# Second block's queries and keys with both input parts as one 512-column operand, and a sum of two banks behind it

## The reference, cut to what matters

```python
h = rms_norm(x, pre_mix_g[l])
z = h @ w_in[l]
za, zb, zc = z[..., :split_a], z[..., split_a:split_b], z[..., split_b:]
ya = spatial_gating(...)                 # from za
q, k, v = jnp.split(zb, 3, axis=-1)      # 512 columns each
yb = moba_attention(q, k, v)             # one block of 256 keys: causal attention with ALiBi
yc = conformer_conv(zc, w_dw[l], ...)    # gated, then a depthwise convolution with 31 taps
y = jnp.concatenate([ya, yb, yc], axis=-1) @ w_out[l]
```

## Time and profile before

| | |
|---|---|
| median of 3 runs | 783.48 us (783.41 to 783.9) |
| the profiled execution | 783.46 us, its span 782.2 us, so 1.26 us around the span |
| PE busy | 769.6 us, 98% |
| PEld, DVE, ACT, POOL busy | 85%, 73%, 56%, 9% |
| mean granted TensorE clock | 0.999 of full speed |

### The profile page before, as it was taken

The page is one execution under the profiler, slowest core; times in us unless marked ns, Lnnn a source line. Parts: engine busy times, 40 slices in busy tenths (PEclk is TensorE's granted clock), DMA queues, the critical chain, the costliest instruction groups (busy, mean ns, idle before and its releaser), DMA issues.

```text
span 782.2 us, 11452 instructions
## 1 busy us (share of the span) xinstructions
PE 769.6 (98%) x4454; PEld 668.2 (85%) x4454; DVE 569.1 (73%) x785; ACT 438.5 (56%) x660; POOL 70.4 (9%) x128
## 2 busy tenths in 40 slices
PE   6999999999999999999999999999999999999996
PEld 5999877888898888888899997789988888888885
DVE  5987999779696666686667998657647656665664
ACT  5555687674665444444465477656646744444452
POOL 4033720000100000000020001110001100000001
PEclk9999999999999999999999999999999999999999
DMA  9999998755367686865556654446434666666651
GB/s 322 368 296 326 358 327 298 292 189 166 116 185 237 211 278 193 272 224 166 183 184 202 184 162 140 157 149 211 153 93 125 213 191 191 192 198 193 189 166 54
DMA packets 84533, 163.34 MB, mean 209 GB/s; under 512 B 5424, under 2 KB 15856, under 8 KB 84480
## 3 DMA queue, kind: packets, MB, share of 16 engines
q1 hardware_dynamic: 82656, 157.31, 61.0%
q10 hardware_dynamic: 1424, 4.81, 1.8%
q0 software_dynamic: 400, 0.50, 0.4%
HBM read 161.55 MB, written 1.05 MB: 208 GB/s over the span
## 4 chain that ended last, share of the span: by engine, by line
PE 96%; ACT 1%; DVE 1%; DMA 1%; issue 1%; SPq 0%; POOL 0%; ACTq 0%; DVEq 0%; POOLq 0%
PE bank L1920 19%; PE bank L1922 19%; PE bank L1921 19%; PE bank L2010 13%; PE bank L2013 7%; PE bank L1982 5%; PE bank L1933 2%; PE bank L1935 1%; PE bank L1940 1%; PE bank L2418 1%; PE bank L2063 1%; PE bank L2721 1%; PE bank L2223 1%; DMA ada_ring<-in_w_ada 1%; DVE ada_acc L1077 1%
## 5 line engine op out<-in xcount | busy, mean ns | idle before, releaser
L1047 DVE TENSOR_TENSOR lo_ring<-raw_ring,hi_ring 128x1024 fp32r<-128x1024 f32 x247 | 302.5, 1230 | 148.3 <-ACT hi_ring L549 147.5
L549 ACT CAST hi_ring<-raw_ring 128x1024 fp32r<-128x1024 f32 x248 | 259.8, 1052 | 255.6 <-PE bank L1922 141.2
L1920 PE MATMUL bank<-hi_ring,branch_hi 128*128 128x512 f32 x352 | 139.2, 395 | 0.0
L1921 PE MATMUL bank<-lo_ring,branch_hi 128*128 128x512 f32 x352 | 137.4, 390 | 0.0
L1922 PE MATMUL bank<-hi_ring,branch_lo 128*128 128x512 f32 x352 | 137.2, 390 | 0.0
L2010 PE MATMUL bank<-h_hi_lo,hi_ring 128*128 128x512 f32 x448 | 111.9, 392 | 0.0
L2010 PEld LDWEIGHTS bank<-h_hi_lo,hi_ring 128*128 128x128 f32 x448 | 81.5, 189 | 15.0
L1922 PEld LDWEIGHTS bank<-hi_ring,branch_lo 128*128 128x128 f32 x352 | 66.1, 188 | 13.9
L1920 PEld LDWEIGHTS bank<-hi_ring,branch_hi 128*128 128x128 f32 x352 | 66.2, 188 | 13.8 <-issue 0.8
L1921 PEld LDWEIGHTS bank<-lo_ring,branch_hi 128*128 128x128 f32 x352 | 66.2, 188 | 13.4 <-issue 0.5
L2013 PEld LDWEIGHTS bank<-h_hi_lo,lo_ring 128*128 128x128 f32 x448 | 61.1, 191 | 4.3
(11 more groups left out here) (323 smaller groups left out, 1208.6 us busy)
## 6 DMA issues: line engine op xcount, KB each, us to landing
raw_ring<-in_w_ff SPq DMA_DIRECT2D x128, 512.0 KB, 3.7
raw_ring<-in_w_in SPq DMA_DIRECT2D x64, 512.0 KB, 5.1
raw_ring<-in_w_out SPq DMA_DIRECT2D x16, 512.0 KB, 3.3
raw_ring<-in_w_xkv SPq DMA_DIRECT2D x16, 512.0 KB, 3.6
mem_v<-in_w_ada SPq DMA_DIRECT2D x13, 512.0 KB, 5.4
mem_k<-in_w_ada SPq DMA_DIRECT2D x11, 512.0 KB, 5.8
ada_ring<-in_w_ada SPq DMA_DIRECT2D x8, 512.0 KB, 6.9
raw_ring<-in_w_branch SPq DMA_DIRECT2D x8, 512.0 KB, 3.6
```

The lines of the kernel that those rows point to most:

```text
L549: act.copy(m.hi[:, m.slot(u)], m.raw[:, m.slot(u)]).then_inc(s.hi_done, 1)
L1047: dve.tensor_tensor(m.lo[:, m.slot(u)], m.raw[:, m.slot(u)], as_f32(m.hi[:, m.slot(u)]), ALU.subtract).then_inc(s.lo_done, 1)
L1920: pe.matmul(out, a_hi, b_hi, start=start, stop=False, skip_group_check=True)
L1921: pe.matmul(out, a_hi, b_lo, start=False, stop=False, skip_group_check=True)
```

## The change

Q2 and K2 go through `unit_both`. Q2 takes banks 2 to 5, K2 banks 0, 1, 6 and 7. ACT copies the high sum out of two banks with each of two instructions (semaphores `q2_part`, `k2_part`), and DVE adds the columns 256:512 in two further instructions, which now count `q2_out` and `k2_out`. DVE's order changes with it: in a slab the first three steps are `after`, five taps, as before; the fourth is five taps, then the two waits and adds, then `after`.

```diff
+Q2_BANKS, K2_BANKS = (2, 4), (0, 6)
...
 (ScalarE)
-    for u0, dst, sem, b0 in ((Q2, m.qT, s.q2_out, 2), (K2, m.kT, s.k2_out, 0)):
+    for u0, dst, sem, tops in ((Q2, m.qT, s.q2_part, Q2_BANKS), (K2, m.kT, s.k2_part, K2_BANKS)):
         for j in range(RING):
             if j == RING - 1:
-                take_half(u0 + RING, b0, pair(dst, 0), sem)
-                take_half(u0 + RING, b0 + 1, pair(dst, 2), sem)
+                act.wait_ge(s.used, u0 + RING)
+                for i, b in enumerate(tops):
+                    act.copy(dst[:, 2 * i:2 * i + 2, :], m.banks[:, b:b + 2, 0:S]).then_inc(sem, 1)
             after(u0 + j)
...
 (VectorE)
-    for j in range(2 * RING):
-        after(Q2 + j)
-        conv_taps(5)
+    for u0, dst, part, done, tops in ((Q2, m.qT, s.q2_part, s.q2_out, Q2_BANKS), (K2, m.kT, s.k2_part, s.k2_out, K2_BANKS)):
+        for j in range(RING):
+            if j == RING - 1:
+                conv_taps(5)
+                for i, b in enumerate(tops):
+                    dve.wait_ge(part, i + 1)
+                    both = dst[:, 2 * i:2 * i + 2, :]
+                    dve.tensor_tensor(both, both, m.banks[:, b:b + 2, S:2 * S], ALU.add).then_inc(done, 1)
+            after(u0 + j)
+            if j < RING - 1:
+                conv_taps(5)
...
 (TensorE)
-    claim(2, 3)
-    for j in range(RING):
-        features(Q2 + j, j, m.h_hi, m.h_lo, 2)
-    free[2] = free[3] = s.q2_out, 2
-    claim(0, 1)
-    for j in range(RING):
-        features(K2 + j, j, m.h_hi, m.h_lo, 0)
-    free[0] = free[1] = s.k2_out, 2
+    for u0, done, tops in ((Q2, s.q2_out, Q2_BANKS), (K2, s.k2_out, K2_BANKS)):
+        for b in tops:
+            claim(b, b + 1)
+        for j in range(RING):
+            unit_both(u0 + j, UK * j, m.h_both, tops, j == 0, j == RING - 1).then_inc(s.used, 1)
+        for i, b in enumerate(tops):
+            free[b] = free[b + 1] = done, i + 1
```

More of the change, by code:

```diff
@@ L310, in __init__ @@
         self.glu, self.glu_sig = new("glu"), new("glu_sig")
+        self.q2_part, self.k2_part = new("q2_high_part"), new("k2_high_part")
         self.q2_out, self.k2_out, self.v2_out = new("q2_out"), new("k2_out"), new("v2_out")
```

## The result

The changed kernel takes 790.41 us (median of 5, 789.55 to 790.66) against 783.48 before: 1.0083 of the time, 95% interval 1.0072 to 1.0095, so 6.9 us slower. The forecast was 787.8, within 787.0 and 790.4; the rival in which the clock falls had 789.6. The clock fell. In the traced execution it cost about what that rival gave it, in the median more.

The account below looks back on a forecast made before the run. PE, busy 98% of the span, was taken to bound the kernel; its scores would now depend on late DVE. 783.46 plus the scores' 4.37 us shift, the 0.68 us product gain lying ahead of the wait, gave 787.8; range 787.0 to 790.4.

Parts of the forecast that it names:

- The new products: PE's eight units of Q2 and K2: 2.795 us each instead of 2.880, saving 0.68 us.
- VectorE's queue: DVE from the first `lo` at 429.46: `lo`s, taps and adds sum to 26.15 us, keys' adds end at 455.61.
- The wait: PE ends unit 142 at 450.57 and idles 5.1 us before the first scores, waiting for DVE's adds.
- the shift of the scores: First scores start at 455.71 instead of 451.34, 4.37 us later, added whole to the kernel's time.
- Nothing given back, no second wait: Behind the first scores, PE and ACT move along; none of the shift recovered (bound 0.5 us), no further DVE wait.
- rival 1: PE's clock falls to 1.2 GHz in the 5.1 us wait, costing 1.75 us more: 789.6; chance 0.38.
- Rivals 2 to 4: The first, rival 2: DVE reaches K2's adds by 449.3, PE doesn't wait, gain stays: 782.8; chance 0.04.
- Rival 3: Behind the scores, DVE runs less late against PE, up to 2 us of the wait come back: 785.8; chance 0.06.
- Rival 4: `unit_both` no faster in Q2 and K2; wait only 4.4 us, time 787.9; chance included in the forecast's 0.50.

Follow-up runs that it names:

- experiment with the dependence alone: Kernel before, old products, no adds; only the second half of the keys copied by VectorE behind all 40 taps instead of ScalarE; 787.65 us, 1.0050 of before.
- the adds at the first free place: Changed kernel with the keys' two adds directly behind lo(144), ten taps following them; 785.67 us, 1.0025 of before.
- the run with the filler: Changed kernel plus 40 unused matmuls of 256 columns between unit 142 and the first scores; 788.11 us, 1.0055 of before.
- the kernel of the deferred taps: Changed kernel with the keys' adds directly behind lo(144) and eight of forty taps moved to later places; 782.91, then 783.08 us (0.9990, 0.9991 of before).

## Why the prediction was right, and where it was short

**The new products.** Forecast 0.68 us for eight units from the pace in the feed-forward layer; measured 0.69 in the trace, and 0.7 to 0.8 in the total where nothing hid it. The Trainium skill ("TensorE: Matmul & The Clock Gate", section "Back-to-back issue gap") would have 0.16; the trace contradicts it here. The Trainium skill itself (same section) calls that formula the gap of a single isolated matmul, and gives about 131 ns at 512 columns for a stream of weight loads and matmuls, as this is. That doesn't fit either: eight matmuls of 512 columns take 427.35 - 425.50 = 1.85 us here, 231 ns each.

**VectorE's queue.** Forecast: 26.15 us from the first `lo` to the end of the adds. Measured: 455.77 - 429.64 = 26.13. The wait was forecast as 5.1 and is 5.02, the shift of the scores as 4.37 and is 4.40 from Q2's start. The four adds themselves cost 2.4 us, about half of the wait. The other half is what the keys' adds had to stand behind, the lateness that VectorE had already, harmless until PE's scores depended on it. The experiment with the dependence alone shows that: one copy of 0.7 us, no add, 3.0 us of wait. In the five kernels that changed what stands ahead of the scores or in the wait, the scores came within 0.3 us of the time counted from the queue.

**Nothing given back, no second wait.** Right for the changed kernel: 326.93 against 326.94 us from the second scores to the end. But the second wait is only covered; it appears when the first gets short (0.68 us with the adds at the first free place).

**The clock.** This is the part that was short. The step that failed is the chance and size of rival 1: "Clock falls, 789.6: 0.38", priced at 1.75. It was given less weight than the 0.50 of a clock that stays up, and it came in all five executions as far as their granted means tell (0.993 to 0.997, against 0.998 to 1.000 of before, with one exception of 0.948); the trace shows it in one. For that one the price was near: 1.54 measured, and 789.55 us against 789.6. In the median the clock cost 2.3 us, by the distance to the run with the filler (788.11), which is the forecast of 787.8 with PE kept at work. I had set the 5.08 us of idle at the start of the span, with a clock of 1.00, against the fall at the end of it; the row at the start told nothing of a wait in the midst of work. The median is at the upper edge of the range, 790.41 against 790.4, for this one reason. That it is no further off is in part luck: the queue, the wait and the shift were worked out and came true, but the path that the forecast of 787.8 stood for did not happen, and the range reached to 790.4 only because it made room for most of the rival.

**Rivals 2 to 4.** That DVE is in time needed 5 us less queue; the kernel that moves eight taps and the adds got there, and its time, 782.9 to 783.1, is the 782.8 of that rival. Rival 3, part recovered, is refuted by the sum of the spans. Rival 4 has no case, since the units were faster. The rival of several experiments, that four banks or 512 columns slow something else, fell with the filler run and with the kernel of the deferred taps.

**Open.** Why the four other executions took 0.4 to 1.1 us more than the traced one isn't seen: only one execution of the changed kernel has a trace, and the others have a mean clock alone. Those of 0.993 and 0.995 would be some 9 and 6 us at the lower level (an estimate: 0.999 less the mean, times 789 us, times two) where the traced one had 3.4. A longer or a second fall is thus likely but not shown. The mean doesn't measure the time lost either: the one execution of before with 0.948 took 784.91 us, only 1.2 more than the median.

## What to carry to other kernels

When a result moves from an engine that keeps up to one that falls behind, price the whole queue ahead of the new instruction, not the instruction: here 2.4 us of adds and a hidden lateness made a wait of 5 us out of a gain of 0.7. Then place the new work first and put off what is not yet needed, and look one dependence further, since a second wait may be covered by the first. On a kernel bound by TensorE a wait of 2 us and more can have a second price in the clock. Taking the wait away was best here (782.9); where that can't be done, other work of TensorE in it is worth much (785.97 with unit 143 in it, against 790.41).

## What the runs showed of the hardware

The clock's fall came after much shorter waits than the end of the span suggested (3.5 us without a matmul): after 3.0 us in two traced executions, and in all in eight of the ten of the two kernels with such a wait (six by mean clock, two by time alone); after 2.1 us in three of six and after 1.1 us in none of nine, both by mean clock. In each of the three traces with a fall it came when PE worked again, in two of them within 0.2 us. In the kernel with the dependence alone PE resumes at 454.63 and the clock falls 1.1 us later:

```profile
455.50:455.75 0.25, 0.25 (x4) 0.25 (x3) 0.19 (x2) 0.00 (x0) 0.00 (x0) 0.97 0.00 0
455.75:456.00 0.25, 0.25 (x3) 0.25 (x3) 0.25 (x2) 0.00 (x0) 0.00 (x0) 0.50 0.00 0
...
459.00:459.25 0.25, 0.25 (x4) 0.25 (x4) 0.25 (x1) 0.00 (x0) 0.00 (x0) 0.70 0.14 41
```

So a wait whose clock row still reads 1.00 is not yet out of it; the windows behind it have to be read too. In the three traces the clock was back at its upper level some 3.4 us after it fell, with PE at work without a gap (456.1 to 459.5 in the changed kernel), and the stretch from the first to the second scores was 1.5 us longer each time.
